# The causal mask of the diagonal score block: added in PSUM by VectorE in place of a TensorE product of identity and mask

## The reference

```python
def attend(args):
    q_blk, blk = args
    s = jnp.einsum('bhqd,bhkd->bhqk', q_blk, kt).astype(jnp.float32) * scale
    q_idx = blk * Q_BLOCK + jnp.arange(Q_BLOCK)
    mask = q_idx[:, None] >= key_idx[None, :]
    s = jnp.where(mask, s, jnp.float32(-1e30))
    pr = jax.nn.softmax(s, axis=-1).astype(vt.dtype)
    return jnp.einsum('bhqk,bhkd->bhqd', pr, vt)
```

## Time and profile before

| what | value |
|---|---|
| time, median of 3 runs | 2486.25 us (2484.96 to 2487.53) |
| the profiled execution's own time | 2483.99 us |
| its span, first to last instruction | 2482.4 us |
| TensorE matmul, share of the span | 98% |
| TensorE weight loads | 77% |
| VectorE | 36% |
| ScalarE, GpSimd | 16%, 16% |
| mean granted TensorE clock | 0.994 |
| `attend`, first to last instruction | about 199 to 398 us of the span |

### The profile page before, as it was taken

How to read it: one execution, slowest core, us unless ns; L and a number is a source line. 1 busy time by engine, 2 the same in 40 slices (tenths; PEclk the granted TensorE clock), 3 DMA queues, 4 the chain that set the end, 5 groups by cost and what they waited for, 6 DMA issues and landing times. The chain is left out here.

```text
span 2482.4 us, 43029 instructions
## 1 busy us (share of the span) xinstructions
PE 2431.1 (98%) x15278; PEld 1910.8 (77%) x15278; DVE 889.5 (36%) x2405; ACT 403.9 (16%) x947; POOL 405.8 (16%) x584
## 2 busy tenths in 40 slices
PE   8998989999999899999999999999999999999999
PEld 6765655444455899999999999999878787887644
DVE  4764673111134532223322333333322232232364
ACT  3334542011011100010101011011000000000133
POOL 2451131221113201100110011011010101111230
PEclk9999999999999999999999999999999999999999
DMA  4000002312073398778778878888999898989462
GB/s 146 26 18 9 1 0 51 119 25 51 4 233 87 117 358 310 263 283 286 274 278 295 296 282 296 311 300 299 325 328 346 322 335 322 335 328 330 170 211 85
DMA packets 240430, 524.65 MB, mean 211 GB/s; under 512 B 14770, under 2 KB 51010, under 8 KB 240355
## 3 DMA queue, kind: packets, MB, share of 16 engines
q1 hardware_dynamic: 213106, 465.48, 53.2%
q0 software_dynamic: 17440, 38.97, 5.0%
q10 hardware_dynamic: 9808, 19.14, 2.0%
HBM read 491.68 MB, written 31.87 MB: 211 GB/s over the span
## 5 line engine op out<-in xcount | busy, mean ns | idle before, releaser
L1612 PEld LDWEIGHTS banks<-arena_a,arena_w 128*128 128x128 f32 x8192 | 966.4, 191 | 8.8 <-issue 6.7
L1612 PE MATMUL banks<-arena_a,arena_w 128*128 128x128 f32 (+8 forms) x8192 | 970.8, 281 | 2.0 <-ACT arena_a L1725 1.6
L1850 DVE TENSOR_SCALAR arena_m<-banks,arena_m 128x160 f32<-128x160 f32 x256 | 98.2, 384 | 599.4 <-PE banks L1612 599.1
L1620 PE MATMUL banks<-arena_a,arena_w 128*128 128x144 f32 (+7 forms) x2304 | 298.0, 286 | 0.2 <-issue 0.2
L1620 PEld LDWEIGHTS banks<-arena_a,arena_w 128*128 128x128 f32 x2304 | 288.2, 190 | 0.5 <-issue 0.4
L1730 ACT ACTIVATE arena_m<-arena_m 128x160 f32<-128x160 f32 x256 | 85.5, 336 | 992.6 <-DVE arena_m L1850 942.3
L1650 PE MATMUL banks<-arena_w,arena_a 128*128 128x512 f32 x448 | 194.6, 592 | 0.0
L1181 POOL DMA_DIRECT2D arena_m<-slot_tokens x32 | 18.6, 580 | 1064.7 <-issue 1064.7
L1650 PEld LDWEIGHTS banks<-arena_w,arena_a 128*128 128x128 f32 x448 | 84.0, 190 | 100.4 <-issue 100.4
L2070 PE MATMUL banks<-arena_h,arena_w 128*128 128x512 f32 (+1 forms) x272 | 111.2, 567 | 0.0
L1869 DVE TENSOR_SCALAR arena_m<-banks,arena_m 128x32 f32<-128x32 f32 x144 | 36.1, 251 | 205.8 <-PE banks L1620 205.8
(11 more groups left out here) (337 smaller groups left out, 2475.7 us busy)
## 6 DMA issues: line engine op xcount, KB each, us to landing
arena_w<-in_w_gate_up_dram SPq DMA_DIRECT2D x128, 2048.0 KB, 12.6
arena_w<-in_w_down_dram SPq DMA_DIRECT2D x32, 4096.0 KB, 15.5
expert_rows<-arena_a ACTq DMA_DIRECT2D x18, 512.0 KB
arena_a<-in_x_dram SPq DMA_DIRECT2D x16, 512.0 KB, 4.1
arena_w<-in_w_in_dram SPq DMA_DIRECT2D x16, 512.0 KB, 5.4
arena_a<-in_b_down_dram SPq DMA_DIRECT2D x14, 512.0 KB, 16.8
expert_rows<-arena_a ACTq DMA_DIRECT2D x28, 192.0 KB
arena_w<-in_w_o_dram SPq DMA_DIRECT2D x1, 4096.0 KB, 14.6
```

The costliest lines, as they stand in the source:

```text
L1612: m = pe.matmul(GU[f % 3][:, to:to + width], w[c][:, k, at:at + P], xT[:, k, 0:width], start=(k == 0), stop=(k == K - 1), skip_group_check ...
L1620: return pe.matmul(DN[d % 2][:, 0:width], wd[:, k, d * P:(d + 1) * P], actT[:, k, 0:width], start=(k == 0), stop=(k == KF - 1), skip_group ...
L1850: dve.tensor_scalar(gc[f % 2], bank[:, 0:WIDTH], bias[:, f:f + 1], SWIGLU_LIMIT, ALU.add, ALU.min).then_inc(sem("gc"), 1)
```

## The change

TensorE's product of identity and mask and the two bf16 constants go. The mask is kept in fp32, and VectorE adds it in place to the diagonal block in PSUM, as a new first instruction of `maxes`; the row maximum waits for that add through a new semaphore `masked`. The last score matmul of a tile increments `scores`. TensorE no longer waits for the constants at its start, VectorE does.

```diff
-                maskb = sb("a_mask", [P, P], BF16, ctx=ctx)
-                identb = sb("a_ident", [P, P], BF16, ctx=ctx)
+                mask = sb("a_mask", [P, P], ctx=ctx)
...
-                        pool.memset(maskb[:, :], 0.0).then_inc(sem("c"), 1)
+                        pool.memset(mask[:, :], 0.0).then_inc(sem("c"), 1)
                         pool.wait_ge(sem("c"), 1)
-                        pool.affine_select(out=maskb[:, :], in_=maskb[:, :], compare_op=ALU.is_ge, fill=NEG, base=0,
+                        pool.affine_select(out=mask[:, :], in_=mask[:, :], compare_op=ALU.is_ge, fill=NEG, base=0,
                                            pattern=[[-1, P]], channel_multiplier=1).then_inc(sem("consts"), 1)
-                        pool.tensor_copy(identb[:, :], ident[:, :]).then_inc(sem("consts"), 1)
...
-                                last = j + w == width
                                 m = pe.matmul(score[s % 2][j // BANK][:, 0:w], qTh[b][0:HD, s * P:(s + 1) * P], kTh[b][0:HD, j:j + w],
-                                              start=True, stop=not last, skip_group_check=True)
-
-                            m = pe.matmul(score[s % 2][s // 4][:, w - P:w], identb[:, :], maskb[:, :], start=False, stop=True,
-                                          skip_group_check=True)
+                                              start=True, stop=True, skip_group_check=True)
                             m.then_inc(sem("scores"), 1)
...
                         def start():
-                            pe.wait_ge(sem("consts"), 2)
...
                             wait_value(dve, sem("scores"), T * h + (s + 1))
+                            own = pairs[s % 2][:, s * P:(s + 1) * P]
+                            dve.tensor_tensor(own, own, mask[:, :], ALU.add).then_inc(sem("masked"), 1)
+                            wait_value(dve, sem("masked"), T * h + (s + 1))
                             dve.tensor_reduce(most[s % 2], pairs[s % 2][:, 0:(s + 1) * P], AX.X, ALU.max).then_inc(sem("m"), 1)
...
                         def start():
+                            dve.wait_ge(sem("consts"), 1)
                             maxes(0, 0)
                             maxes(0, 1)
```

## The result

The changed kernel took 2492.78 us in the median of 9 runs (2489.16 to 2496.75), the kernel before 2487.53 us in the median of 9 (2484.95 to 2490.48). The ratio on record is 1.0025 (the two medians alone give 1.0021), with a 95% interval of 1.0015 to 1.0034: slower by some 4 to 8 us. The forecast of 2489.8 was on the right side and too small; the range of 2484 to 2497 holds the result. Of the 3.0 us between 2489.8 and 2492.78, 1.3 are not the change's: the kernel before came out at 2487.53 here and at 2486.25 in the runs that the forecast started from.

A forecast was written before the change was run, and what follows sets the result against it. Hand-overs between TensorE and VectorE were taken to bound the stage: 0.6 us in each of five loop heads (3.0) plus 0.5 in head 7 made 3.5 us, so 2486.25 + 3.5 = 2489.8 us, range 2484 to 2497.

The forecast's parts named there:

- What bounds the stage: In the edited stage, neither TensorE nor VectorE alone sets the pace; a loop of hand-overs from scores to next scores does.
- The product: On TensorE, each of 64 removed mask products saves 0.06 us, 3.8 us in all; its semaphore comes 0.06 earlier.
- The add: On VectorE, each of 64 new PSUM adds takes 0.29 us (0.27 to 0.41), plus 0.12 until the row maximum.
- 0.6 us a head: Each of loop heads 1 to 5 gets 0.6 us longer through later norms and transposes, 3.0 us in all.
- the transposes of tile 4 start at 311.48 instead of 311.22: 0.26: Within a loop head, TensorE's tile 4 transposes follow norm(4) by 0.34 us and so start 0.26 later.
- Head 6 gives nothing: Head 6 gets no longer, because GpSimd's differences already hold VectorE's norms there.
- Heads 0 and 7: Head 0 set at zero, its start's savings against two early adds; head 7 0.5 us for two tight hand-overs.
- The sum: Whole kernel: 3.0 us from loop heads plus 0.5 from head 7, 3.5 us slower, giving 2489.8 us.
- The falling clock: Longer TensorE idle before tile 6 halves its clock, about 1.5 us a stretch; 2493 to 2497 us; chance 0.14.
- The collision of norm(2): VectorE's norm(2) is held by a GpSimd copy, 0.8 us more a head; 2493.8 us; chance 0.13.
- the slow rivals: Two slower cases, TensorE's clock falling and norm(2) meeting a GpSimd copy; chance 0.27 together.
- The fast rival: Each removed product saves TensorE up to 0.33 us instead of 0.06, so the kernel gets faster, 2483 us; chance 0.08.

The follow-up runs named there:

- third profile: The changed kernel run a third time, unaltered, beside the kernel before: 2494.39 us, ratio 1.0038.
- experiment 1: The kernel before with TensorE's mask product kept and an add of zeros, with its wait, put on VectorE: 2495.81 us, ratio 1.0037.

## Why the prediction was right, point by point

- **What bounds the stage.** Right: neither engine alone, but the hand-overs. Lengthened by 0.40 us with the product kept, a head takes 24.0 us; shortened by 0.26 us, 22.45; without mask work 22.71.
- **The product: 0.06 us on TensorE, 0.06 of semaphore.** Right in size, as far as the runs tell. Taking it out without an add saves 0.3 us a head, as was expected from these two figures before that run.
- **The add: 0.29 and a wait of 0.12.** Measured 0.30 and 0.10.
- **0.6 us a head.** Mis-sized: 0.79, and 1.03 in the first of the five. The step that failed is "the transposes of tile 4 start at 311.48 instead of 311.22: 0.26". They start 0.45 later. The prediction had them wait for norm(4), 0.34 behind its end. The wait that ends last there is another: for s = 4 TensorE also waits for ScalarE's last copy of the next head's queries and keys (line 904), which the list of waits in "The kernel before" leaves out. The rows had a sign of it, 0.42 behind norm(4) and not 0.34. The copy stands behind the exponential of tile 5, and so behind row maximum 5: it ends at 310.92 before and at 341.17 in the changed kernel, 0.45 later, and the transposes follow it by 0.30 in both. There is no slack of 0.08 at this place; the whole lateness of row maximum 5 passes. That makes 0.26 into some 0.34. The rest is that norm(1) was 0.41 late instead of 0.35 (the reciprocal ahead of it started 0.27 behind the copy of the transposed tile, not 0.21), which through TensorE's next scores made tile 3 late by 0.43 instead of 0.33. Row maximum 7 then added its 0.34, and tile 6 was 0.78 late instead of 0.61.
- **Head 6 gives nothing.** Right: 30.17 us before, 30.29 to 30.31 in the three profiles of the changed kernel. GpSimd's differences still hold its norms.
- **Heads 0 and 7.** Zero and 0.5 us were forecast, and the profiles don't separate them from the clock. Head 0 ends 0.3 us later in two profiles (227.49 and 227.47 against 227.16), one with the 10.2 us of half clock of the kernel before, the other with 6.8, and 1.5 later in the one with 13.7. Head 7 takes 0.2, 1.6 and 0.6 us more, with 0.8, 4.0 and 1.8 us of half clock in it against 1.5 before.
- **The sum.** With 0.79 in place of 0.6 the loop heads give 4.2 and the whole 5.3 us (third profile, last norm(7) at 398.77 against 393.45, no half clock in heads 1 to 5). The medians of the three measurements lie 5.3, 7.6 and 7.4 us above the kernel before beside them. What lies above 5.3 us is at least in part clock.
- **The rivals.** The falling clock (0.14) came beside the forecast, in two heads of the profiled execution. These are 1.4 and 1.7 us longer, for two stretches and one held norm(2); with 0.57 us for the latter, as in experiment 1, a stretch cost some 1.3 us, an estimate (1.5 predicted). The collision of norm(2) (0.57 us, 0.8 predicted) came there once, and in three heads of experiment 1, in the fourth head without any half clock. Both had been weighed as alternatives; they are additions to it, each of which comes in some heads. That, 0.79 for 0.6, and the 1.3 us by which the kernel before came out higher, are why 2489.8 was too low. It is also why "slower", with 0.37, should have had more of the chance than "within 0.2%": the measured ratio is 1.0025, just outside, and the forecast by itself, 2489 to 2492, did not hold 2492.78; the range did, with the room it made for the slow rivals. The fast rival is out: at its 0.33 a product, heads without product and add would have been shorter by 0.8 us or more, and they are by 0.3.

## What to carry to other kernels

An instruction that comes behind a wait is not covered by that wait: VectorE was busy for a third of the time and waited 67 us for scores, and 0.40 us more in each hand-over still lengthened each head by 0.8. List every wait of an instruction before you take one as the last: here a third engine's copy stood between two that were followed closely. Count the time from one engine's end to the other's start along the loop, not the shares; and look for work to take out of the hand-over, as a scale that can be applied to an operand beforehand. When an edit lengthens an idle time of TensorE, look at the granted clock and at GpSimd's copies of several executions before giving a cause to one profile's extra microseconds.

## What the runs showed of the hardware

- TensorE's clock fell to 1.2 GHz behind idle times as short as 1.48 to 1.58 us in an otherwise busy stretch (3 of 20 heads) and behind 1.99 us in 4 of 5; with 0.81 to 1.28 us it did not, in 30 heads.
- An fp32 add of 128x128 in place in PSUM takes 0.30 us (0.284 to 0.300 in all 64), where the adds with an output in SBUF, carried on to 128 columns, give 0.27.
- A VectorE tensor_scalar in SBUF that started 0.05 us ahead of a GpSimd copy was held to the copy's end (0.42 us became 1.08); one that started 0.11 ahead (310.46 against 310.57 in the changed kernel) took its 0.42.
- A wait takes longer in the loop, where its target is in a register, than in the unrolled heads, where it is a constant: from the end of norm(6) to the start of its transposes 0.34 us in the loop, 0.05 in head 7 (before: 391.91 to 391.96); from ScalarE's copy to the transposes of tile 4, 0.30 in the loop, 0.06 in head 0. The runs don't separate the register from the loop.
